# Seven re-orderings in a chain of transformer blocks: high parts first in the norms, a factor ahead of the maxima in every second attention work, the mixer's triangle ahead of a bank's copy

## The reference, cut to what matters

```
for i in range(2):                                  # first block
    sh1, sc1, g1, sh2, sc2, g2 = split(silu(c) @ ada_w[i] + ada_b[i], 6)
    h = rms_norm(x) * (1 + sc1) + sh1
    y = nsa_mixer(h) if i == 0 else swa_sink_mixer(h)
    x = x + (1 + g1) * rms_norm(y)
    h = rms_norm(x) * (1 + sc2) + sh2
    y = square(relu(h @ w_up)) @ w_down              # 1024 -> 4096 -> 1024
    x = x + (1 + g2) * rms_norm(y)
# second block
x = x + hybrid_mixer(rms_norm(x))        # pooling and a gated linear attention in chunks of 64
x = x + memory_cross_attention(rms_norm(x), rms_norm(mem))
u = causal_conv3(rms_norm(x) @ w_up)     # 1024 -> 2 * 2816
x = x + (silu(u[..., :2816]) * u[..., 2816:]) @ w_down
return rms_norm(x)
```

## Time and profile before

| | |
|---|---|
| median of 3 runs (lowest to highest) | 2088.24 us (2086.16 to 2090.5) |
| the profiled execution's own time | 2093.22 us |
| its span | 2091.4 us |
| mean granted clock of TensorE | 0.974 |
| busy: TensorE, VectorE, GpSimd, ScalarE | 1979.1, 1130.6, 945.0, 696.4 us |
| chain that ended last, by engine | PE 70%, issue 12%, POOL 7%, DVE 7%, ACT 3%, DMA 1% |

### The profile page before, as it was taken

One profiled execution on the slowest core, in us unless ns is written; L12 is line 12 of the kernel. 1 busy time (PEld: TensorE's weight loads), 2 busy tenths in 40 slices (PEclk: granted clock), 3 DMA queues, 4 the chain that ended last, 5 costly groups with the idle time before them and its releaser, 6 DMA issues.

```text
span 2091.4 us, 26683 instructions
## 1 busy us (share of the span) xinstructions
PE 1979.1 (95%) x10120; PEld 1619.7 (77%) x10120; DVE 1130.6 (54%) x1729; ACT 696.4 (33%) x1217; POOL 945.0 (45%) x552
## 2 busy tenths in 40 slices
PE   6998999899999999888999999899999989999997
PEld 5887776678888877766888888787897778788885
DVE  7566775873554667656322313785463339546163
ACT  3343554332222233544322223342343322222122
POOL 1464554365444445544444444542373235344442
PEclk9999999899999999999999999998999999999998
DMA  7774331445555415512323223221342213223221
GB/s 287 237 217 155 107 97 63 179 150 193 192 176 197 160 60 164 164 66 71 101 91 101 93 99 94 68 81 61 101 141 81 71 61 110 91 91 100 92 100 60
DMA packets 79986, 252.18 MB, mean 121 GB/s; under 512 B 12160, under 2 KB 12672, under 8 KB 79616
## 3 DMA queue, kind: packets, MB, share of 16 engines
q1 hardware_dynamic: 79872, 250.61, 35.9%
HBM read 235.21 MB, written 15.37 MB: 120 GB/s over the span
## 4 chain that ended last, share of the span: by engine, by line
PE 70%; issue 12%; POOL 7%; DVE 7%; ACT 3%; DMA 1%; SPq 0%; POOLq 0%; DVEq 0%; ACTq 0%
PE ps L901 19%; PE ps L903 19%; PE ps L902 19%; POOL wl L793 5%; PE ps L1153 3%; PE ps L1125 2%; PE ps L1087 1%; ACT pr L2556 1%; DVE st L1862 1%; PE ps L1419 1%; POOL al L849 1%; PE ps L1444 1%; PE ps L964 1%; POOL x L841 1%; PE ps L965 1%
## 5 line engine op out<-in xcount | busy, mean ns | idle before, releaser
L793 POOL TENSOR_TENSOR wl<-raw,wh 128x1024 fp32r<-128x1024 f32 x309 | 769.8, 2497 | 987.4 <-ACT wh L2411 987.3
L2411 ACT CAST wh<-raw 128x1024 fp32r<-128x1024 f32 x309 | 322.3, 1049 | 925.6 <-PE ps L903 850.7
L901 PE MATMUL ps<-ah,wh 128*128 128x512 f32 x1240 | 489.8, 395 | 1.1 <-DVE pair L1794 1.1
L902 PE MATMUL ps<-ah,wl 128*128 128x512 f32 x1240 | 484.4, 391 | 0.0
L903 PE MATMUL ps<-al,wh 128*128 128x512 f32 x1240 | 484.3, 391 | 0.0
L901 PE MATMUL ps<-hh,wh 128*128 128x512 f32 x688 | 271.5, 395 | 5.4 <-DVE hl L2368 5.4
L901 PEld LDWEIGHTS ps<-ah,wh 128*128 128x128 f32 x1240 | 234.0, 189 | 53.3 <-issue 4.0
L902 PEld LDWEIGHTS ps<-ah,wl 128*128 128x128 f32 x1240 | 233.7, 188 | 49.8 <-issue 1.8
L903 PEld LDWEIGHTS ps<-al,wh 128*128 128x128 f32 x1240 | 233.7, 189 | 49.4
L903 PE MATMUL ps<-hl,wh 128*128 128x512 f32 x688 | 270.5, 393 | 0.0
L902 PE MATMUL ps<-hh,wl 128*128 128x512 f32 x688 | 268.9, 391 | 0.0
(11 more groups left out here) (377 smaller groups left out, 2857.3 us busy)
## 6 DMA issues: line engine op xcount, KB each, us to landing
raw<-in_units SPq DMA_DIRECT2D x309, 512.0 KB, 3.5
ada_mlp<-in_ada SPq DMA_DIRECT2D x64, 512.0 KB, 3.3
ada<-in_ada SPq DMA_DIRECT2D x16, 512.0 KB, 15.8
qs<-qscr SPq DMA_DIRECT2D x32, 256.0 KB, 3.5
ada_in<-in_ada SPq DMA_DIRECT2D x16, 512.0 KB, 3.4
ks<-kscr SPq DMA_DIRECT2D x24, 256.0 KB, 4.7
x<-in_xT SPq DMA_DIRECT2D x1, 2048.0 KB, 12.8
qscr<-rot_h SPq DMA_DIRECT2D x16, 128.0 KB, 2.4
```

Of the source, the lines that this page charges most:

```text
L793: nc.gpsimd.tensor_tensor(wl[:, slot], raw[:, slot], wh[:, slot].bitcast(F32), ALU.subtract).then_inc(lo_done, 1)
L901: nc.tensor.matmul(out_ap, wh[:, slot, k], high[:, k0 + k], start=first and k == 0, stop=False)
L902: nc.tensor.matmul(out_ap, wl[:, slot, k], high[:, k0 + k], start=False, stop=False)
L2411: a.copy(wh[:, slot], raw[:, slot]).then_inc(hi_done, 1)
```

## The change

Seven edits, all in the order of instructions or in a tile's place; no matrix product is left out.

1. `gemm_first` waits for the high part of a chunk, does the six matmuls with it, then waits for the low part and does the other three. All six norms use it.
2. In `norm_shared` with a residual, `to_add(1)` stands ahead of `scaled(0)`.
3. In the first attention, query blocks 0 and 2 of a work get a mask matmul each (128 columns) where one of 256 columns served both.
4. In nsa_out, `ada_late` stands behind unit 5 in place of 4, `ada_turn` behind 7 in place of 6, `ada_fold` behind bank 6 in place of 5.
5. In the second attention, in even steps t of VectorE's loop the factor of work t-1 stands ahead of the maxima of work t (t = 4 to 14; the two first works lie ahead of the loop).
6. In the mixer, the triangle and the low part stand ahead of the bank's copy.
7. In the ffn, the Silu writes to PSUM bank 5 or 6, and VectorE's product reads that bank and one SBUF tile where it read two SBUF tiles.

```diff
-        def gemm_first(first, high, low, ready):
+        def gemm_first(first, high, low, name):
...
-                pe.wait_ge(*ready[k])
+                pe.wait_ge(high_made, DC * NORMS.index(name) + k + 1)
                 for j in range(3):
                     o, slot = ps[:, (n + j) % RING], (first + j) % RING
                     nc.tensor.matmul(o, wh[:, slot, k], high[:, k], start=k == 0, stop=False)
                     nc.tensor.matmul(o, wl[:, slot, k], high[:, k], start=False, stop=False)
+                pe.wait_ge(*A_READY[name][k])
+                for j in range(3):
+                    o, slot = ps[:, (n + j) % RING], (first + j) % RING
                     mm = nc.tensor.matmul(o, wh[:, slot, k], low[:, k], start=False, stop=k == DC - 1)
...
-                    elif plan.nsa and i == 0:
-                        mm = nc.tensor.matmul(ps[:, bank, col - P:col + P], ident_r[:],
-                                              mask_r[:, 1:2].to_broadcast([P, 2, P]), start=False, stop=True)
-                    elif plan.nsa or i == 0:
+                    if plan.nsa or i == 0:
                         mm = nc.tensor.matmul(o[:, width - P:width], ident_r[:], mask_r[:, 1], start=False, stop=True)
...
-                     between=lambda c: ada_late(0) if c == 4 else ada_turn(0) if c == 6 else None)
+                     between=lambda c: ada_late(0) if c == 5 else ada_turn(0) if c == 7 else None)
...
                 add(0)
+                to_add(1)
                 scaled(0)
-                to_add(1)
                 low(0)
...
-                if t < len(works):
+                if t < len(works) and not plan.nsa and t % 2 == 0:
+                    last()
+                    maxima(t, lambda: None)
+                elif t < len(works):
                     maxima(t, last)
...
-        pb = {2: bank()}
-        link(v.tensor_copy(po[:, 2], pb[2]))
         dve.wait_ge(sct_read, 1)
...
         v.tensor_tensor(ol[:, 3], po[:, 3], oh[:, 3].bitcast(F32), ALU.subtract)
+        pb = {2: bank()}
+        link(v.tensor_copy(po[:, 2], pb[2]))
         dve.wait_ge(chunk_kv, 1)
...
-                            link(v.tensor_tensor(uc[:, j // 2, 1], uc[:, j // 2, 0], uc[:, j // 2, 1], ALU.mult))
+                            link(v.tensor_tensor(uc[:, j // 2, 1], ps[:, 5 + j // 2], uc[:, j // 2, 1], ALU.mult))
...
-                a.activation(o, o, ACT.Silu).then_inc(conv_silu, 1)
+                a.activation(ps[:, 5 + c % 2], o, ACT.Silu).then_inc(conv_silu, 1)
```

More of the change, by code:

```diff
@@ L1085, in score @@
                     o = ps[:, bank, col:col + width]
-                    for part in range(1 if plan.nsa and i == 2 else 2):
+                    for part in range(2):
                         nc.tensor.matmul(o, qs[:, Q_SLOT[j], i * P:(i + 1) * P], ks[:, slot, part, k0 * P:k1 * P],
[L1088 to L1091, removed]
-                    elif plan.nsa and i == 0:
-                        mm = nc.tensor.matmul(ps[:, bank, col - P:col + P], ident_r[:],
-                                              mask_r[:, 1:2].to_broadcast([P, 2, P]), start=False, stop=True)
-                    elif plan.nsa or i == 0:
+                                         start=part == 0, stop=False)
+                    if plan.nsa or i == 0:
                         mm = nc.tensor.matmul(o[:, width - P:width], ident_r[:], mask_r[:, 1], start=False, stop=True)
@@ L1208, in mlp @@
                     if b == 0:
-                        gemm_first(u, ah, al, A_READY[name])
+                        gemm_first(u, ah, al, name)
                     else:
@@ L1252, in _ @@
         u = FIRST["nsa_in"]
-        gemm_first(u, ah, al, A_READY["nsa_in"])
+        gemm_first(u, ah, al, "nsa_in")
         gemm(u + 3, RING - 3, ah, al)
@@ L1297, in _ @@
         gemm_squared(FIRST["nsa_out"], ah, al, ready=(o_split, 0), adds=True,
-                     between=lambda c: ada_late(0) if c == 4 else ada_turn(0) if c == 6 else None)
+                     between=lambda c: ada_late(0) if c == 5 else ada_turn(0) if c == 7 else None)
         mlp("mlp0", 0)
-        gemm_first(FIRST["swa_in"], ah, al, A_READY["swa_in"])
+        gemm_first(FIRST["swa_in"], ah, al, "swa_in")
         gemm(FIRST["swa_in"] + 3, 1, ah, al)
@@ L1311, in _ @@
         u = FIRST["mix_in"]
-        gemm_first(u, ah, al, A_READY["mix_in"])
+        gemm_first(u, ah, al, "mix_in")
         pe.wait_ge(evac, done[0] - 2)
@@ L1487, in _ @@
                 if grp == 0:
-                    gemm_first(u, ah, al, A_READY["ffn"])
+                    gemm_first(u, ah, al, "ffn")
                     gemm(u + 3, 2 * n - 3, ah, al)
@@ L2107, in _ @@
         ada_coef(0, 4)
-        squared_out(lambda c: v.tensor_copy(y[:, c], bank()), lambda c: ada_fold(0) if c == 5 else [ada_step(n) for n in (2 * c, 2 * c + 1) if n < 8],
+        squared_out(lambda c: v.tensor_copy(y[:, c], bank()), lambda c: ada_fold(0) if c == 6 else [ada_step(n) for n in (2 * c, 2 * c + 1) if n < 8],
                     factor=coef_at(0, 2))
```

## The result

| | before | changed |
|---|---|---|
| median of 8 runs each (lowest to highest) | 2087.41 us (2082.51 to 2091.93) | 2072.60 us (2066.90 to 2079.13) |
| ratio, 95% interval | | 0.9930 (0.9912 to 0.9949) |
| span of the profiled execution | 2091.4 us | 2073.5 us |

The kernel became 14.6 us faster (10.6 to 18.4 by the interval); 2076 was forecast, with 2070 to 2085 as the range. The spans of the two profiled executions are 17.9 us apart: these executions took 2093.22 and 2075.32 us, which is 5.8 and 2.7 over the medians of the table.

What follows compares the result with a forecast made beforehand. PE, busy 95% of the span, was taken as the bound. Norms -4.3, masks +2.6, nsa_out -4.0, second attention 0, mixer -1.8, ffn -5.0 sum to -12.5: 2088.24 to 2075.7, forecast 2076 us; 8-in-10 range 2070 to 2085.

Steps and rivals of the forecast that it cites:

- the ffn: Ffn: 22 VectorE products some 0.65 us shorter each, waits and low clock behind the first group reduced: -5.0 us.
- the rival of moved stalls: Ffn: the product's gain turns into longer copies and low parts, -1.4 in place of -5.0, total 2079.5 us; chance 0.15.
- nsa_out: nsa_out: `ada_late`'s 1.98 us wait and the low clock behind it go, `ada_turn` moves into waiting time: -4.0 us.
- the mixer's wait: Mixer: recurrence starts some 3 us sooner, covering PE's 1.81 wait: -1.8 us; up to -3.5 with the clock.
- the norms of mlp0: Norms, high parts first: mlp0 -1.4, mlp1 -0.8, ffn -0.8 us; all six norms sum to -4.3.
- the factor at 0: Second attention: maxima 1.6 us later, even copy late by 0.4 at most, taken up by PE's 1.49 wait: 0.
- the slower rival: Second attention: even works' chain becomes what PE waits for, six steps of 3.25, +19.5 us, total 2095.5; chance 0.10.
- the masks' term: First attention: 32 added mask matmuls at 0.11 us each cost +3.5 at most, +1.0 at least; taken +2.6 us.
- Mix_in's loss: mix_in: -0.8 from the norm, +0.7 for the exposed gate copy, +0.6 for the later chain to pooling: +0.5 us.
- the moved `to_add(1)`: Norms: costs nothing in mlp0 and swa_in, where VectorE idles 0.85 us; about 0.6 in mlp1 and mix_in.
- swa_in, of the same form: -1.4: swa_in's norm: high parts first win the same as in mlp0, -1.4 us.
- The rival of a low clock that comes back: Low clock returns elsewhere, keeping 1.65 us each in nsa_out and ffn; masks +3.5, norms -1.5; total 2083; chance 0.17.

Runs made afterwards that it cites:

- the SBUF variant: Kernel before, but the ffn's Silu writes to its own SBUF tile, which VectorE's product reads with another SBUF operand: 2087.47 us, +1.5 (-1.3 to +4.4).
- b3_no_swa_mask_mix: Changed kernel with swa_in's and mix_in's first products as before and the first attention's masks merged as before: 2069.77 us, ratio 0.9917.
- b1 to b3: Changed kernel with swa_in's first products as before; then also the first attention's masks; then also mix_in's first products: 2070.53, 2068.58, 2069.77 us.
- b1_no_swa: Changed kernel, but swa_in's first products take a unit's three products together as before: 2070.53 us, ratio 0.9929.

## Why the prediction was right, point by point

The stretches, from the start of one matmul to that of another, in us; in the profiles of the single edits and of before, without an edit of theirs, and in the two profiles of the changed kernel:

| stretch | without the edit | changed | forecast |
|---|---|---|---|
| nsa_out to the root behind it | 50.4 to 52.0 | 48.1, 48.1 | -4.0 |
| root to first down unit, mlp0 | 54.5 to 55.3 | 53.9, 53.6 | -1.4 |
| root to end of the norm's units, swa_in | 32.9 to 33.6 | 32.2, 31.9 | -1.4 |
| from there to the attention's projection | 108.3 to 111.9 | 117.9, 119.3 | 0 |
| root to first down unit, mlp1 | 54.6 to 55.4 | 53.7, 53.7 | -0.8 |
| mix_in's root to the gates' transposes | 70.1 to 71.0 | 71.5, 71.4 | +0.5 |
| chunk products to head products | 9.5 | 7.6, 7.6 | -1.8 |
| head products to their squares | 29.4 to 32.7 | 27.8, 27.8 | 0 |
| ffn's root to its first down unit | 93.1 to 93.3 | 92.5, 89.9 | -0.8 |
| first group's down units | 48.2 to 48.3 | 44.4, 44.4 | -3.9 |
| rest of the ffn to the last root | 236.5 to 236.6 | 235.3, 235.2 | -1.2 |

Right, in place and size: the ffn (-5.2 in its profile, -4.8 by the runs, for -5.0), with the rival of moved stalls refuted by its own lines and the operand's place shown by the SBUF variant; nsa_out (-4.0 by the runs; in the profiles -3.1 in the mean, since the low clock that the step counts as going with the wait was behind it in only four of eight); the mixer's wait (-1.88 for -1.8, the recurrence 2.9 sooner for some 3); the norms of mlp0 (-1.2 in the mean for -1.4), mlp1 and ffn; the factor at 0 by the mechanism that was given: the even copy 1.6 later, the even turn 0.4 later, the odd wait 0.4 shorter, and a cycle of 7.81 as before, so that the slower rival, that chain becoming the bound, did not come.

Mis-sized: the masks' term, +2.6, measured about +1.2. The price of a matmul was right, 0.10 a work for the 0.11 of the row; what was too small is the part that is hidden behind waits for ScalarE. Mix_in's loss has the right sign, +1.1 for +0.5 in the mean, but part of that is half clock; with 10.2 us of it on both sides the stretch is 0.4 to 1.1 longer, and 0.5 to 0.6 longer than in b3_no_swa_mask_mix. And the moved `to_add(1)` is not free in every execution: the idle time of VectorE ahead of `scaled(0)`, 0.85 in the earlier trace rows, is 0.10 in swa_in where the clock is full at that point, and PE's first product there comes 6.66 behind the root in the changed kernel's second profile and 6.20 in the one with swa_in's high parts alone.

Failed: the step "swa_in, of the same form: -1.4". The form is the same and the 1.4 came, but behind mlp0's units comes dense work of PE, behind swa_in's come stores, loads and rotary that PE's lead does not move. There PE met its DMA wait sooner (2.43 and 2.91 in place of 0.60): the first scores stand 56.8 and 57.0 behind the root, in the kernels before 55.6 to 56.9, so the lead was gone there. At that wait the clock fell to half, and VectorE's subtraction landed beside GpSimd; in both profiles the stretch is 6 to 11 us longer. Not all of that is swa_in's high parts: with these alone put back (b1 to b3) it takes 111.4 to 113.1, still 2 to 4 over 109.6, the mean of the seven profiles without any edit of the norms, and what that rest comes from stays open. The step asked what the norm's wait hides, not what waits next.

What hid this in the sum is a term that the sum did not have: the half clock in the mixer's heads, about 2.8 less in the mean (the mixer's step had -3.5 as its far end), with the 1.4 that the masks cost less. That these cancel is luck: the sum is right though one step failed, one was mis-sized and one was missing. The rival of a low clock that comes back had the right kind of thing in the wrong place.

The differences of the stretches, those not listed too, come to -9.7 us from the mean of the kernels without an edit to the mean of the changed kernel's two profiles, the runs to -14.6. Most of that gap is the choice of executions: the two profiled ones took 2.7 and 6.0 us more than the medians of their runs (2075.32 and 2077.02 against 2072.60 and 2071.02), while the nine of before and the single edits lie from 5.7 under to 5.8 over theirs, and on them in the mean. The clock says the same: of the first eight runs the three slowest have a mean granted clock of 0.977 to 0.978, the five others 0.980 to 0.983. So the long entry, seen in both profiles, need not be in most executions; how often it comes was not measured, as only profiled executions show it. That also fits b1_no_swa, which mends it in its profile and not in the median.

## What to carry to other kernels

In mlp0 and mlp1, where dense work of the bounding engine follows, the lead that was won was kept; in swa_in, ahead of a DMA and another engine's chain, it became a longer wait, with half clock behind it. So each place of an edit that is used six times needs its own next wait. VectorE's product of two SBUF operands, which shared its time with GpSimd's weight work, was mended by one operand in PSUM. Compare stretches over several kernels before putting down a difference of one profile to an edit: from nsa_in's first product to nsa_out's the time at half clock was 10.2 us in one profile of the changed kernel and 20.5 in the other.

## What the runs showed of the hardware that was not expected

The same stretch of the same instructions ran at the granted clock of 0.50 for 10.2 to 17.1 us (the mixer's heads, eight profiles without the edit), and behind the same idle of 1.97 to 1.98 us in nsa_out the clock fell in four profiles and stayed up in four; behind an idle of 2.18 in the ffn of the kernel before (2047.60) it stayed full. VectorE's product with one operand in PSUM took 691 to 693 ns in all 22 instances, 21 of them beside GpSimd's weight work; with both in SBUF, 691 to 2585.
